# Second attention's output product and second down product with tokens on the partitions

## What is computed

```
mod = silu(c) @ ada_w + ada_b               # sh1, sc1, g1, sh2, sc2, g2
h = rmsnorm(x, mix_norm_pre) * (1 + sc1) + sh1
q, k, v = split(h @ w_qkv)
out = windowed_attention_with_sink(q, k, v) # (512, 1024)
y = out @ w_o
x = x + g1 * rmsnorm(y, mix_norm_post)
h = rmsnorm(x, ffn_norm_pre) * (1 + sc2) + sh2
a, b = split(h @ w_in)                      # 2816 wide each
y = (silu(a) * b) @ w_out
x = x + g2 * rmsnorm(y, ffn_norm_post)
```

## Time and profile before

| | us |
|---|---|
| median of 3 runs (1502.03 to 1504.06) | 1503.44 |
| the profiled execution, whole | 1502.69 |
| its span, first to last instruction | 1500.4 |
| PE busy | 1392.5 (93%) |
| POOL, DVE, ACT busy | 639.0, 622.6, 557.7 |
| q, k, v product of the second block | from 877.3 to 946.5 |
| second attention | to 1047.4 |
| output product | 1047.4 to 1091.2 |
| from there to the first matmul of the up product | to 1119.8 |
| up product | to 1362.0 |
| down product | to 1482.6 |
| the end | to 1500.4 |

### The profile page before, as it was taken

One profiled execution on the slowest core, in us unless ns is written; L12 is line 12 of the kernel. 1 busy time (PEld: TensorE's weight loads), 2 busy tenths in 40 slices (PEclk: granted clock), 3 DMA queues, 4 the chain that ended last, 5 costly groups with the idle time before them and its releaser, 6 DMA issues.

```text
span 1500.4 us, 17375 instructions
## 1 busy us (share of the span) xinstructions
PE 1392.5 (93%) x6384; PEld 1118.6 (75%) x6384; DVE 622.6 (41%) x1093; ACT 557.7 (37%) x815; POOL 639.0 (43%) x516
## 2 busy tenths in 40 slices
PE   8899997898678899999999989899979999999995
PEld 1788876786676678888888878655868888888884
DVE  3544578576842543434343352575241000002124
ACT  3512313563322543444422442576243322323230
POOL 0343353134633345444465744433434454445542
PEclk9999997899989899999999989999959999999998
DMA  9234553500012155445433423100111323222221
GB/s 394 88 113 168 196 196 100 150 1 1 1 57 112 53 200 219 173 190 201 168 140 112 139 90 108 57 1 1 56 56 57 112 84 110 85 97 99 84 85 56
DMA packets 26981, 165.48 MB, mean 110 GB/s; under 512 B 2688, under 2 KB 4992, under 8 KB 8496
## 3 DMA queue, kind: packets, MB, share of 16 engines
q1 hardware_dynamic: 24912, 150.10, 27.4%
q10 hardware_dynamic: 2016, 14.68, 2.8%
HBM read 162.64 MB, written 6.32 MB: 113 GB/s over the span
## 4 chain that ended last, share of the span: by engine, by line
PE 82%; DVE 6%; POOL 4%; issue 3%; ACT 3%; DMA 1%; POOLq 0%; SPq 0%; ACTq 0%; DVEq 0%
PE bank L246 54%; PE bank L287 10%; PE bank L1129 3%; PE bank L604 2%; PE bank L584 2%; PE bank L465 2%; POOL arena L782 1%; PE bank L1106 1%; POOL w_lo L239 1%; DMA w_raw<-w_dram 1%; PE bank L1189 1%; POOL arena L784 1%; PE bank L594 1%; PE bank L444 1%; PE bank L445 1%
## 5 line engine op out<-in xcount | busy, mean ns | idle before, releaser
L239 POOL TENSOR_TENSOR w_lo<-w_raw,w_hi 128x512 fp32r<-128x512 f32 x368 | 504.2, 1402 | 669.3 <-ACT w_hi L230 669.3
L246 PE MATMUL bank<-h_hi,w_hi 128*128 128x512 f32 x1248 | 495.3, 397 | 24.4 <-POOL w_lo L239 9.8
L246 PE MATMUL bank<-h_lo,w_hi 128*128 128x512 f32 x1248 | 490.5, 393 | 0.0
L246 PE MATMUL bank<-h_hi,w_lo 128*128 128x512 f32 x1248 | 490.2, 393 | 0.0
L230 ACT ACTIVATE w_hi<-w_raw 128x2048 fp32r<-128x2048 f32 x92 | 176.2, 1915 | 382.2 <-PE bank L246 198.1
L246 PEld LDWEIGHTS bank<-h_hi,w_hi 128*128 128x128 f32 x1248 | 237.8, 191 | 76.8 <-issue 22.9
L246 PEld LDWEIGHTS bank<-h_hi,w_lo 128*128 128x128 f32 x1248 | 237.2, 190 | 50.1
L246 PEld LDWEIGHTS bank<-h_lo,w_hi 128*128 128x128 f32 x1248 | 237.8, 191 | 49.2
L1825 DVE TENSOR_TENSOR arena<-arena,bank 128x512 f32 (+1 forms) x22 | 15.1, 687 | 209.4 <-PE bank L246 209.4
L287 PE MATMUL bank<-h_hi,w_hi 128*128 128x512 f32 x224 | 87.2, 389 | 0.0
L287 PE MATMUL bank<-h_hi,w_lo 128*128 128x512 f32 x224 | 87.2, 389 | 0.0
(11 more groups left out here) (229 smaller groups left out, 1641.2 us busy)
## 6 DMA issues: line engine op xcount, KB each, us to landing
w_raw<-w_dram SPq DMA_DIRECT2D x92, 1024.0 KB, 4.8
ada_ring<-ada_dram SPq DMA_DIRECT2D x30, 1024.0 KB, 4.8
ada_ring<-ada_dram ACTq DMA_DIRECT2D x14, 1024.0 KB, 4.8
arena<-ada_dram SPq DMA_DIRECT2D x4, 1024.0 KB, 10.7
arena<-x_dram SPq DMA_DIRECT2D x2, 2048.0 KB, 11.6
bias_copies<-bias_rows SPq DMA_DIRECT2D x1, 4096.0 KB, 25.2
arena<-bias_copies SPq DMA_DIRECT2D x1, 3072.0 KB, 13.6
out_dram<-arena SPq DMA_DIRECT2D x8, 256.0 KB, 2.1
```

Source lines behind the costliest of these rows:

```text
L239: last = nc.gpsimd.tensor_tensor(w_lo[b % 2][:, part], w_raw[b % 2][:, part], w_hi[b % 2][:, part], ALU.subtract)
L246: last = nc.tensor.matmul(bank[:, :], w[:, ft, k, :], x[:, k, :], start=k == first and m == 0, stop=k == final and m == 2)
```

## The change

- **Output product and down product** now take the activations (a 128x128 piece: 128 features of 128 tokens) as the stationary operand and the weights (128 features x 512 outputs) as the moving one (`row_product`). A bank then holds 128 tokens of 512 outputs: token tile t uses banks 2t and 2t+1. The number of matmuls of each width is the same. The weights are arranged in the host accordingly.
- **The last two blocks** of each product are run token tile by token tile (`last_rows`), so tile 0 is complete while tiles 1 to 3 are still to be done.
- **Statistic of a token tile**: ACT squares a bank and sums along the free dimension in the same instruction (`y_statistic`), so no PE work is needed. DVE scales (`add_row`), POOL adds the left half of the residual and DVE the right one. `x_statistic` and `normalise_row` do the same for the statistic of x and scale it into XN.
- **The residual is turned once** during the q, k, v product (`turn_residual`, 32 PE transposes, 8 copies on ACT), and the two post-norm rows are made there too (16 fp32 matmuls with the identity, 4 copies). XN is turned back for the up product by 32 transposes (`turn_normed`), 16 before the first up matmul and 16 within the first block's chunks.
- **Three blocks set aside**: 57 and 58 (rounded parts in the arena region of attention's keys and bias, once the attention is over) and 91. `high` and `low` of these do not wait for a slot to be used up.
- **Output** is written as (token tile, half), 8 pieces of 256 KB as before.

```diff
+        def high_aside(act, b):
+            act.wait_ge(raw_in[b % 2], 16 * (b // 2 + 1))
+            nc.scalar.activation(aside[b][0], w_raw[b % 2][:], ACT.Copy).then_inc(hi_done, 1)
+        def low_aside(pool, b):
+            pool.wait_ge(hi_done, b + 1)
...
+        def row_product(w, slot, k, t, h, start, stop):
+            part, cols = slice(t * P, t * P + P), slice(512 * h, 512 * h + 512)
+            for m, (x, n) in enumerate(((h_hi, 0), (h_lo, 0), (h_hi, 1))):
+                last = nc.tensor.matmul(ps[2 * t + h][:, :], x[:, slot + k, part], w[n][:, k, cols], start=start and m == 0, stop=stop and m == 2)
+            return last
+        def last_rows(pe, blocks, slots):
+            for t in range(4):
+                for h in range(2):
+                    for b, slot in zip(blocks, slots):
+                        w = row_weights(b)
+                        for k in range(2):
+                            last = row_product(w, slot, k, t, h, False, b == blocks[-1] and k == 1)
...
+                    last.then_inc(o_done, 1)
...
-            rest(B_QKV, F_QKV, 3)
+            for f in range(4):
+                turn_residual(f)
+            one_tile(B_QKV, F_QKV, 4)
+            one_tile(B_QKV, F_QKV, 5)
+            for f in range(4, DC):
+                turn_residual(f)
+            one_tile(B_QKV, F_QKV, 6)
+            one_tile(B_QKV, F_QKV, 7)
...
+            def lead_turned():
+                pe.wait_ge(o_scaled, 6)
+                pe.wait_ge(xn_left, 3)
+                pe.wait_ge(xn_right, 3)
+                turn_normed(0, (0, 1, 2))
+                turn_normed(1, (0, 1, 2))
+                pe.wait_ge(o_scaled, 8)
+                turn_normed(2, (0, 1, 2))
+                turn_normed(3, (0, 1, 2))
+                pe.wait_ge(xn_left, 4)
+                pe.wait_ge(xn_right, 4)
+                for f in range(4):
+                    turn_normed(f, (3,)).then_inc(xn_done, 1)
+                pe.wait_ge(lo_done, B_UP2 + 1)
+                for k in range(DC):
+                    pe.wait_ge(h_low, 24 + k + 1)
+                    if k + 4 < DC:
+                        turn_normed(k + 4, range(4)).then_inc(xn_done, 1)
+                    for ft in (0, 1):
+                        last = chunk_products(B_UP2, ft, ps[ft], k)
...
+            def down_rows(b0, g0, bank_free):
...
+                whole(8)
+                pe.wait_ge(g_split, g0 + 11)
+                pe.wait_ge(lo_done, b0 + 11)
+                last_rows(pe, (b0 + 9, b0 + 10), (2, 4))
...
             attention2_act(act)
             sqrt_table()
+            act.wait_ge(at2["olo"], 2 * NG)
+            high_aside(act, 57)
+            high_aside(act, 58)
+            high(act, 59, used=56)
+            high(act, 60, used=57)
+            def y_statistic(q, t):
+                for h in range(2):
+                    act.wait_ge(o_done, 2 * q + h + 1)
+                    col = 2 * t + h
+                    nc.scalar.activation(junk[:, h, :], ps[col][:, :], ACT.Square, accum_out=y_part[:, col:col + 1]).then_inc(o_sq, 1)
+                act.wait_ge(o_sq, 2 * q + 2)
+                act.wait_ge(o_bias, q + 1)
+                nc.scalar.activation(y_inverse[:, t:t + 1], y_part[:, 2 * t + 1:2 * t + 2], ACT.Sqrt, ...)
+            def x_statistic(t):
+                act.wait_ge(add_left, t + 1)
+                nc.scalar.activation(junk[:, 0, :], XRT[:, t, 0:512], ACT.Square, accum_out=...).then_inc(x_left, 1)
+                act.wait_ge(x_left, t + 1)
+                act.wait_ge(x_bias, t + 1)
+                nc.scalar.activation(x_inverse[:, t:t + 1], ..., ACT.Sqrt, ...).then_inc(x_root, 1)
+                act.wait_ge(x_inv, t + 1)
+                nc.scalar.activation(XN[:, t, 512:D], XRT[:, t, 512:D], ACT.Copy, scale=x_inverse[:, t:t + 1]).then_inc(xn_right, 1)
+            for t in range(4):
+                y_statistic(t, t)
+                x_statistic(t)
...
+            act.wait_ge(half_used, 2 * B_DOWN2 + 14)
+            hidden_high(slice(16, 18), 0)
+            high(act, B_DOWN2 + 9)
+            act.wait_ge(half_used, 2 * B_DOWN2 + 16)
+            hidden_high(slice(18, 20), 2)
+            hidden_high(slice(20, 22), 4)
+            high_aside(act, B_DOWN2 + 10)
+            sqrt_table()
+            for t in range(4):
+                y_statistic(4 + t, t)
...
+            def add_row(q, t, post):
+                dve.wait_ge(o_sq, 2 * q + 1)
+                nc.vector.tensor_scalar(y_mean[:, t:t + 1], y_part[:, 2 * t:2 * t + 1], 1.0 / D, EPS, ALU.mult, ALU.add).then_inc(o_bias, 1)
+                dve.wait_ge(o_root, q + 1)
+                nc.vector.reciprocal(y_inverse[:, t:t + 1], y_inverse[:, t:t + 1]).then_inc(o_inv, 1)
...
+                for h in range(2):
+                    nc.vector.scalar_tensor_tensor(out=turn_sum[:, t % 2, half], in0=ps[2 * t + h][:, :], scalar=y_inverse[:, t:t + 1],
+                                                   in1=post[:, half], op0=ALU.mult, op1=ALU.mult).then_inc(o_scaled, 1)
+                nc.vector.tensor_tensor(XRT[:, t, 512:D], XRT[:, t, 512:D], turn_sum[:, t % 2, 512:D], ALU.add).then_inc(add_right, 1)
+            def normalise_row(t):
+                nc.vector.tensor_tensor_reduce(out=turn_sum[:, t % 2, 512:D], in0=right, in1=right, ..., accum_out=...).then_inc(x_right, 1)
+                nc.vector.tensor_scalar(x_mean[:, t:t + 1], ...).then_inc(x_bias, 1)
+                dve.wait_ge(x_root, t + 1)
+                nc.vector.reciprocal(x_inverse[:, t:t + 1], x_inverse[:, t:t + 1]).then_inc(x_inv, 1)
+                nc.vector.tensor_scalar(XN[:, t, 0:512], XRT[:, t, 0:512], x_inverse[:, t:t + 1], None, ALU.mult).then_inc(xn_left, 1)
```

More of the change, by code:

```diff
@@ L117, in build @@
         ysq_buf = sb("y_squares", [P, S])
+        wdt_hi, wdt_lo = sb("w_dt_hi", [P, DC * 16], F32R), sb("w_dt_lo", [P, DC * 16], F32R)
+        with nc.sbuf_tensor("arena", [P, ARENA], F32) as arena:
+            pass
+        sb("arena_start", [P, A_OVER])
+        over = sb("arena_rounded", [P, 12288], F32R)
+        sb("arena_end", [P, ARENA - A_OVER - 12288])
         def view(tensor, at, *dims):
@@ L207, in build @@
                                 arena[0:16, A_CON2 + 1024:A_CON2 + 1536])
+        aside = {b: (over[:, at:at + BLK], over[:, at + BLK:at + 2 * BLK]) for b, at in A_ASIDE.items()}
+        def high_aside(act, b):
[3 more added lines that the diff above has]
+            pool.wait_ge(hi_done, b + 1)
+            for q in range(4):
+                part = slice(q * 512, q * 512 + 512)
+                last = nc.gpsimd.tensor_tensor(aside[b][1][:, part], w_raw[b % 2][:, part], aside[b][0][:, part], ALU.subtract)
+            last.then_inc(lo_done, 1)
         def load_ada(eng, src, c, off=0):
@@ L372, in spread, with affine @@
             return last
-        def affine(act, m, gain, shift, xn, hb, aside=None):
+        def affine(act, m, gain, shift, xn, hb, aside=None, turned=None):
             for c in range(DC):
@@ L1305, in _ @@
             pe.wait_ge(v2_free, 4)
-            pe.wait_ge(tile_free, F_O)
+            pe.wait_ge(tile_free, F_UP2)
             attention2_pe(pe)
             pe.wait_ge(at2["olo"], 2 * NG)
-            tiles(B_O, F_O, 2)
-            mean_head(pe, 4, SQ2, 4)
-            mean_last(pe, 4, SQ2, 4)
-            spread(pe, 4, 4).then_inc(scale_out, 1)
-            for f in range(DC):
-                pe.wait_ge(sq_done, 40 + f + 1)
-                for t in range(4):
-                    last = nc.tensor.matmul(ps[5][:, t:t + 1], SQ2[:, f % 2, t * P:(t + 1) * P], con_("mean")[:, 0:1],
-                                            start=f == 0 and t == 0, stop=f == DC - 1 and t == 3)
-                    if t == 2 and f == DC - 1:
-                        last.then_inc(sq_used, 1)
-                last.then_inc(sq_used if f < DC - 1 else mean_done, 1)
@@ L1321, in _, with output_products @@
-            spread(pe, 5, 5).then_inc(scale_out, 1)
-            pe.wait_ge(tile_free, F_UP2)
-            lead(pe, B_UP2, 24)
+            def output_products():
+                for j in range(2):
+                    pe.wait_ge(lo_done, B_O + j + 1)
+                    w = row_weights(B_O + j)
+                    for k in range(2):
+                        for t in range(4):
+                            for h in range(2):
+                                last = row_product(w, 2 * j, k, t, h, j == 0 and k == 0, False)
+                        last.then_inc(half_used, 1)
+                pe.wait_ge(lo_done, B_O + 4)
+                last_rows(pe, (B_O + 2, B_O + 3), (4, 6))
@@ new lines, in _ @@
+            for t in range(4):
+                y_statistic(t, t)
+                x_statistic(t)
+            affine(act, 3, lambda c: gain4[:, c:c + 1], lambda c: mod2[:, 24 + c:25 + c], None, HB2, turned=lambda c: ps[4 + c % 4][:, :])
+            glu(B_UP2, F_UP2, False, 2)
+            act.wait_ge(tile_free, F_UP2 + 44)
+            high(act, B_DOWN2 + 2)
```

(24 more changed lines are left out.)

220 lines of the change are left out of this document (145 added, 75 removed).

## The result

The changed kernel takes 1488.19 us (median of 4 runs, 1486.99 to 1489.3), the kernel before beside it 1503.75 (4 runs, 1502.03 to 1505.48): ratio 0.9896, 95% interval 0.9879 to 0.9914. The forecast was 1488.3. The profiled execution took 1488.21 with a span of 1486.4, 14.0 under the 1500.4 of before.

What follows compares the result with a forecast made beforehand. PE was taken as the bound, 82% of the span, with gaps before the up product and at the end to shorten. Terms +7.1 - 14.9 + 4.2 - 11.5 = -15.1 took 1502.69 to 1487.6; plus 0.75, 1488.3 us, range 1482.5 to 1496.0.

Steps and rivals of the forecast that it cites:

- Turning the residual and the rows: In the q, k, v product: 32 transposes and 16 fp32 matmuls paid in full on PE, +7.1 us.
- Output to up product: Gap between these products: 28.6 us go, 11.9 of tile chain and 1.8 of transposes replace them, -14.9 us.
- the low clock at the start of the up product is paid before and after: Start of the up product: low clock costs the same in both kernels, so no term for it.
- The tile's period set by ACT's order: Before the up product: next tile's squares queue behind ACT's scaling, so a tile takes 6.54 us, not PE's 5.44.
- The cover of blocks 57 and 58, at nothing: Output product: weights set aside early are ready 12 us in, needed 21.8 us in, so they cost nothing.
- Block 60 on POOL ends as the first left sum is due: End of the output product: POOL finishes block 60 some 15 us before the last matmul, so no wait.
- Down product, 3.3 + 1.7 - 0.8: Before the last two down blocks: PE wait 3.3, clock fall 1.7, old sums removed 0.8; together +4.2 us.
- Rival 1: Down product: no wait before the last rows (1483.3 us), or one without clock fall (1486.6); chance 0.18.
- The end, -11.5: After the down product: 17.8 us go and 6.3 replace them, the last 2.5 after the sums; -11.5 us.
- Rival 2: Token tiles' chain: a tile takes 7.8 us instead of 6.54, giving 1493.3 us; chance 0.16.
- Rival 3: Output and down products: swapped operands make row products dearer, 0.245 instead of 0.228 us, giving 1500.5; chance 0.06.
- Rival 4: Token tiles' chain over ACT and DVE becomes the bound, 11.5 us per tile, giving 1508.1 us; chance 0.05.

Runs made afterwards that it cites:

- e5: Changed kernel with only a quarter of the residual's transposes and of the post-norm rows' fp32 matmuls; median 1481.84 us, ratio 0.9862 to the kernel before.
- e3: Changed kernel with ACT squaring the next tile's first bank before the square of x; median 1485.42 us, ratio 0.9868 to the kernel before.
- e4: Changed kernel with block 58's rounding held until blocks 55 and 56 are used up; median 1498.11 us, ratio 0.9952 to the kernel before.
- e1: Changed kernel with block 90 set aside as well, not waiting for a slot; median 1482.14 us, ratio 0.9853 to the kernel before.
- e2: Changed kernel with hidden chunks 20, 21 split before block 90 is rounded; median 1485.96 us, ratio 0.9871 to the kernel before.

## Why the prediction was right, point by point

- *Turning the residual and the rows, +7.1.* Measured +6.8: the three groups are 7.07, the piece of 48 before them has no wait, and the attention was 0.3 shorter. e5 confirms that the price is PE's own time.
- *Output to up product, -14.9.* Measured -14.6, and 13.5 us from the last output row product (1098.80) to the first up matmul (1112.29), where I had 11.9. XN was complete 9.8 us after the last matmul, not 9.15: the single chain is 6.2 instead of 5.85 long (reads and small operations; the root took 0.29, not 0.2), and the period 6.64 instead of 6.54. The handovers with four transposes at half pace took 3.7 instead of 2.8. That is 1.6 more in all. Two things take most of it back. Four of the 16 transposes are within these 3.7, so 1.4 instead of 1.8 us of them are left behind the first up matmul: -0.4. The other is the step "the low clock at the start of the up product is paid before and after", which failed: before, matmuls ran at 0.50 for 5.6 us (from 1119.77 to the return at 1125.4), after for 3.6, which gives 1.0 back. -14.9 + 1.6 - 0.4 - 1.0 is -14.7. So the mechanism held, and that this part came out within 0.3 is in part luck. The clock's return in the kernel before:

```profile
1125.00:1126.00 1.00, 1.00 (x5) 0.81 (x4) 0.97 (x2) 1.00 (x2) 0.00 (x0) 0.80 0.00 0
```

- *The tile's period set by ACT's order.* Shown by e3, at the predicted 0.6 us per tile.
- *The cover of blocks 57 and 58, at nothing.* Held, and e4 gives its worth, 10 us. "Block 60 on POOL ends as the first left sum is due" was near: 1084.15 and 1084.59. There was 0.44 us to spare. The 10 us are for block 58 alone; block 57 was not tried.
- *Down product, 3.3 + 1.7 - 0.8.* The wait was 3.29, the fall cost 1.65; e1, with neither, is at 119.69, 0.9 below the 120.6 of before, which is the removed sums and some 0.1 of the product. Rival 1 was wrong for this kernel as it stands, but half right: the wait can leave the clock alone, as e3 and e4 had it, and I had put the fall down as if the length of the wait decided it. That the fall came in the changed kernel, as forecast, is thus in part luck. (The fall in the earlier trace rows that it was taken from stood at 278.9 by its row, not 278.95.)
- *The end, -11.5.* Measured -11.4. The chain goes over DVE's right sum, which ends at 1483.85, 0.55 us after POOL's left sum beside it, and from there to the span's end at 1486.40, 2.55 us, taken as 2.5.
- *Rival 2 (7.8 us per tile)*: 6.64. *Rival 3 (dearer row products)*: 87.05 us for 384 are 0.2267 each, so swapping the operands cost nothing. *Rival 4*: no handover in the chain of waits is over 0.15 us. Most are 0.02 to 0.05, as the prediction had them; those from ACT or DVE to PE are 0.14, which it had at 0.03.

## What to carry to other kernels

Before a matmul that needs a late weight block, ask when its buffer comes free, not only how long the rounding takes: the 5.2 us here came from block 90 having to wait for a slot, and a buffer already idle took them away. Where tiles pass through a chain over two engines, put the part of the next tile that has its input already into the gaps of the present one; and when an earlier start falls into a stretch of low clock, count only what is left of it (0.9 of 1.7 us here). Compare small edits from a common instruction just ahead of them, since medians here moved by more than the edits were worth.

## What the runs showed of the hardware

A wait of 3.3 us before the same 96 matmuls cost 1.65 us more in five executions and nothing in two, without a difference in its length; the fall stood 341.3 us after the clock's last return in all five. A wait of 2.3 us was followed by no fall, in e2 as in the earlier trace rows. DVE's 128x512 sum of two SBUF operands, begun 0.6 us after POOL's, took 1.20 us instead of 0.69 and ended about half a microsecond after POOL's, so splitting such a sum over the two engines gains 0.1 us of a tile's 6.7. ACT's square with a running sum has a read of 0.19 behind it, but the next square begins 0.56 after the first, before the read has ended, so that read is covered. A 128x128 fp32 transpose took 0.109 us of PE, a 128-column fp32 matmul with the identity 0.22.
